# Low halves of the first three state-space input panels moved from GpSimd to VectorE

## The reference

```python
h = rmsnorm(x, norm_mix[l])
proj = h @ w_in[l]
(z, xbc, dt_raw, lru_y, lru_x, q, k, v, ret_g, gate_pre) = jnp.split(proj, offsets, axis=-1)
...
y_lru = rglru_mixer(lru_y, lru_x, ...)      # r, i = sigmoid(xb @ w_a), sigmoid(xb @ w_i); h = scan(a, u); h * gelu(y)
...
# ssd_mixer
xbc = jax.nn.silu(causal_dwconv(xbc, conv_w, conv_b))
```

## Time and profile before

| what | value |
| --- | --- |
| median of 3 runs | 2905.98 us (2905.45 to 2906.31) |
| the profiled execution | 2905.02 us, its span 2903.1 us |
| TensorE | 2878.9 us busy (99%), 17526 matmuls |
| VectorE | 2190.7 us busy (75%) |
| ScalarE | 1382.2 us busy (48%) |
| GpSimd | 396.9 us busy (14%) |

### The profile page before, as it was taken

How to read it: one execution, slowest core, us unless ns; L and a number is a source line. 1 busy time by engine, 2 the same in 40 slices (tenths; PEclk the granted TensorE clock), 3 DMA queues, 4 the chain that set the end, 5 groups by cost and what they waited for, 6 DMA issues and landing times.

```text
span 2903.1 us, 49040 instructions
## 1 busy us (share of the span) xinstructions
PE 2878.9 (99%) x17526; PEld 2533.8 (87%) x17526; DVE 2190.7 (75%) x3578; ACT 1382.2 (48%) x2252; POOL 396.9 (14%) x320
## 2 busy tenths in 40 slices
PE   9999999999999999999999999999999999999999
PEld 7888788778999888998887899988998887699987
DVE  8797574667999868887566888848889767688862
ACT  4653732344655525555233655525555236465541
POOL 0043240001111001110033011001110021011100
PEclk9999999999999999999999999999999999999999
DMA  3222123225677326773334477436773232257723
GB/s 139 100 92 91 66 94 116 73 80 181 156 184 180 89 94 181 181 180 100 109 109 131 128 180 181 113 116 178 185 182 106 103 115 74 81 157 183 183 78 109
DMA packets 143715, 375.93 MB, mean 129 GB/s; under 512 B 16144, under 2 KB 16400, under 8 KB 143184
## 3 DMA queue, kind: packets, MB, share of 16 engines
q1 hardware_dynamic: 110160, 309.44, 31.5%
q0 software_dynamic: 33408, 64.50, 13.1%
HBM read 371.78 MB, written 2.10 MB: 129 GB/s over the span
## 4 chain that ended last, share of the span: by engine, by line
PE 91%; DVE 6%; ACT 2%; issue 1%; DMA 1%; POOL 0%; SPq 0%; DVEq 0%; ACTq 0%; POOLq 0%
PE ps L1033 17%; PE ps L1035 17%; PE ps L1034 17%; PE ps L1487 12%; PE ps L1489 12%; PE ps L1488 12%; PE ps L1430 1%; DVE w_lo L2646 1%; DVE region_low L3216 0%; PE ps L1713 0%; PE ps L1750 0%; PE ps L1205 0%; DVE region_low L3589 0%; PE ps L1194 0%; PE ps L1419 0%
## 5 line engine op out<-in xcount | busy, mean ns | idle before, releaser
L1824 ACT ACTIVATE w_hi<-raw 128x1024 fp32r<-128x1024 f32 x300 | 315.8, 1055 | 284.3 <-DMA raw<-in_wstream 284.1
L1487 PE MATMUL ps<-h_hi,w_hi 128*128 128x256 f32 x1440 | 409.6, 284 | 1.1 <-DVE h_lo L3296 0.4
L1488 PE MATMUL ps<-h_lo,w_hi 128*128 128x256 f32 x1440 | 407.5, 283 | 0.0
L1033 PE MATMUL ps<-h_hi,w_hi 128*128 128x512 f32 (+1 forms) x883 | 347.4, 393 | 2.6 <-DVE w_lo L2646 1.8
L1035 PE MATMUL ps<-h_hi,w_lo 128*128 128x512 f32 (+1 forms) x883 | 340.7, 386 | 0.0
L1034 PE MATMUL ps<-h_lo,w_hi 128*128 128x512 f32 (+1 forms) x883 | 340.5, 386 | 0.0
L2646 DVE TENSOR_TENSOR w_lo<-raw,w_hi 128x1024 fp32r<-128x1024 f32 x220 | 265.7, 1220 | 84.7 <-ACT w_hi L1824 74.3
L1487 PEld LDWEIGHTS ps<-h_hi,w_hi 128*128 128x128 f32 x1440 | 276.1, 192 | 6.2 <-issue 1.6
L1488 PEld LDWEIGHTS ps<-h_lo,w_hi 128*128 128x128 f32 x1440 | 276.2, 192 | 0.5 <-issue 0.2
L937 POOL TENSOR_TENSOR w_lo<-raw,w_hi 128x1024 fp32r<-128x1024 f32 x78 | 195.2, 2508 | 496.6 <-ACT w_hi L1824 487.2
L1833 ACT ACTIVATE stage<-ps 128x512 f32<-128x512 f32 x107 | 63.4, 596 | 393.3 <-PE ps L1035 380.1
(11 more groups left out here) (694 smaller groups left out, 7635.7 us busy)
## 6 DMA issues: line engine op xcount, KB each, us to landing
raw<-in_wstream SPq DMA_DIRECT2D x301, 512.0 KB, 3.2
region<-in_pairs SPq DMA_DIRECT2D x193, 256.0 KB, 4.0
region<-in_pairs POOLq DMA_DIRECT2D x124, 256.0 KB, 5.5
region<-in_pairs SPq DMA_DIRECT2D x46, 512.0 KB, 5.8
last_pairs<-in_pairs SPq DMA_DIRECT2D x66, 256.0 KB, 4.0
raw<-in_pairs SPq DMA_DIRECT2D x22, 512.0 KB, 5.0
last_pairs<-in_pairs SPq DMA_DIRECT2D x22, 512.0 KB, 5.5
last_pairs<-in_pairs POOLq DMA_DIRECT2D x44, 256.0 KB, 5.5
```

The costliest lines, as they stand in the source:

```text
L1033: nc.tensor.matmul(dst, hi_w, hi_x, start=first, stop=False)
L1487: nc.tensor.matmul(dst, w1, x1, start=start, stop=False, skip_group_check=not first)
L1488: nc.tensor.matmul(dst, w1, x0, start=False, stop=False, skip_group_check=not first)
L1824: nc.scalar.activation(w_hi[:, n % HL], raw[:, r], ACT.Copy).then_inc(hi_ready, 1)
```

## The change

The first GpSimd run begins at panel 31 instead of 28. VectorE therefore makes the low halves of panels 28, 29 and 30. Because one pass of the `xbc` loop would then have panels of both makers, the three passes are written out on TensorE and on VectorE. ScalarE and SyncE have the same instructions as before.

```diff
-POOL_RUNS = {"first": (ST["xbc"].n, ST["br0"].n),
+POOL_RUNS = {"first": (ST["xbc"].n + 3, ST["br0"].n),
...
-            gemm("xbc", h_hi, h_lo)
+            gemm("xbc", h_hi, h_lo, groups=(0, 1, 2))
...
-            gemm("xbc", ssd_in, 3)
+            gemm("xbc", ssd_in, 3, groups=(0, 1, 2))
```

## The result

The changed kernel takes **2913.93 us** (median of 10 runs, 2911.49 to 2916.51), the kernel before 2906.31 us (10 runs beside them). The ratio is 1.0026, 95% interval 1.0018 to 1.0034: 7.6 us slower, just over the 0.2% that a measurement can tell. In a second series it took 2912.59 us (11 runs) against 2906.17, ratio 1.0023 (1.0014 to 1.0032). The forecast was 2914.0 us, in the range 2909.8 to 2916.0.

What follows compares the result with a forecast made beforehand. TensorE, busy 99% of the span, was taken as the bound. Panel 29's shift of +6.20, 0.17 for restarting and 1.7 for the clock sum to +8.07 on 2905.98: 2914.0 us, range 2909.8 to 2916.0.

Steps and rivals of the forecast that it cites:

- The old wait: TensorE's 1.77 us idle before panel 27, blamed on GpSimd's panel 28 lengthening VectorE's chain by 2.19 us; claimed to vanish.
- panel 28: Low half made by VectorE in the last block: ready at 163.70, wanted at 164.40, so hidden by 0.7 us.
- panel 29: Low half behind the recurrence's last result: VectorE's turn at 174.75, TensorE wants it at 169.84; the deciding term.
- The race: GpSimd's panel 32 asks at 174.62, VectorE's panel 29 at 174.75; GpSimd first by 0.13 us, a margin as large as the error.
- rival 1: VectorE's panel 29 goes ahead of GpSimd's panel 32: +4.25 + 1.7 = +5.95 us, 2911.9; chance 0.30.
- the forecast's case: GpSimd's panel 32 goes ahead of VectorE's panel 29: +6.37 + 1.7 = +8.07 us, 2914.0; chance 0.42.
- The clock term: TensorE's clock drops to the lower level after the new gap at panel 29: 1.7 us lost, ends 0 and 3.4.
- the restart: TensorE's slow restart after a wait, 0.17 us as seen at panel 27, added to panel 29's shift.
- The rival without a clock loss: TensorE's clock stays up after the gap at panel 29: +4.25 or +6.37 us, 2910.2 or 2912.3; chance 0.10.
- The prediction's row at 8.00: At 8.00 to 10.70 TensorE was busy 1.60 of 2.70 us, then granted clock 0.51 for 3.40 us: 1.7 us lost.
- Panel 30: Low half behind tile 0's convolution, 4.4 us after panel 29's, 6.5 with a lock; panel 29's 5.44 plus 1.7 hides it.
- Rival 3: Not slower: TensorE doesn't wait at panel 29 and the wait before panel 27 is gone: 2903.4 us; chance 0.06.

Runs made afterwards that it cites:

- The kernel with the loops alone: The kernel before with only the xbc loops written out on TensorE and VectorE, all low halves as before: 2906.78 us against 2906.25, ratio 1.0002.
- The forcing kernels: The changed kernel with panel 29's low half made to precede GpSimd's panel 32: 2912.19 us against 2906.30; with the order reversed: 2914.59 against 2906.17.
- the filled gap: The changed kernel with VectorE always first, plus 22 unused TensorE products ahead of its wait for panel 29: 2909.98 us against 2906.30, ratio 1.0015.

## Why the prediction came out as it did

**The mechanism was right.** The old wait went for the reason given (line 2976 at 0.69 us instead of 2.88), panel 28 was hidden (its low half began at 162.28, forecast 162.48), and panel 29 decided. VectorE's turn for it came at 174.45, forecast 174.75, or 174.56 with this execution's 0.19. The rest of the difference is mostly the one lock in this chain: priced at 2.13, it took 2.04 us (3.26 - 1.22). GpSimd asked at 168.96 and 174.45, forecast 169.1 and 174.62. Nothing later took the delay back. The kernel with the loops alone rules out the written-out code.

**The race was called the wrong way for the executions that the profiles show.** The forecast gave GpSimd the first place, by a margin of 0.13 us that it called as large as its error. All three profiles of the change have VectorE first, as in rival 1. In the first the margin was 0.00: the 0.09 us by which the lock was priced too high is most of the 0.13. The forcing kernels bracket it: +5.9 and +8.4 us against the +5.95 and +8.07 of the two cases. The median of the first series, +7.6, lies between them and nearer to the forecast's case, that of the second series, +6.4, nearer to rival 1. So that the first median came within 0.1 us of the forecast is partly luck: the case behind the number is not the one that the profiles show, and no profile shows what happened in the runs around that median.

**The clock term was right in kind and in range, on weak grounds.** It was set at 1.7 us, with ends at 0 and 3.4, plus 0.17 for the restart. From panel 29's start to the next wait it was 130.58 us before. The three profiles of the change have 133.18, 132.29 (174.41 to 306.70) and 132.22 (174.30 to 306.52), so they lose 2.60, 1.71 and 1.64 us. With VectorE forced first it is 132.83 (175.51 to 308.34), a loss of 2.25, and with GpSimd forced first 133.53 (178.12 to 311.65), a loss of 2.95. The low half of panel 29 moved early gives the smallest loss: from panel 30's start it was 125.14 us before (177.38 to 302.52) and is 126.64 (183.66 to 310.30), 1.50 more. The length of the gap doesn't order these losses: 2.95 stands behind 3.87 and 8.24 us, 1.50 behind 8.74, and 1.64 to 2.60 behind the same 5.91. What differs is how much of the time at 1.2 GHz falls on work. In the first profile the clock falls at about 174 and is back at 181.0, 5.3 us after panel 29's start, and half of that is 2.6. In the third it falls at about 171 and is back at 177.6, 3.3 us after the start, and half of that is 1.6. In the first profile 3.98 + 2.60 gives the whole 6.58. The rival without a clock loss is out: only the filled gap keeps its clock, and it is 2.2 us faster.

*TensorE: Matmul & The Clock Gate* of the Trainium skill ("Why this matters for your kernels") says that a long enough gap sends TensorE back to its throttled clock, and the traces agree (0.50 behind 3.87 us and more). The prediction's row at 8.00 was weaker evidence for it than I took it to be. These are TensorE's idle times in and just before that row, and at 985 to 989, in the kernel before:

```profile
8.87 0.47 PE L1033 MATMUL ps<-br_hi,w_hi 128*128 128x512 f32 x1 [1.36 <-DVE br_lo L2871]
...
10.04 0.50 PE L1033 MATMUL ps<-br_hi,w_hi 128*128 128x512 f32 x1 [0.24 <-DVE br_lo L2871]
...
988.66 0.50 PE L1033 MATMUL ps<-region_low,w_hi 128*128 128x512 f32 x1 [2.56 <-DVE region_low L3589]
```

The clock fell at 10.70 behind idle times of 1.36 and 0.24 us and stayed up behind 2.56. So the length of a gap alone doesn't tell the two rows apart, the row at 8.00 is no case of a long gap, and the 1.7 us taken from it were a guess at the price. That it came out inside 1.50 to 2.95 is in part luck.

**Panel 30** was hidden as forecast, but closely: the filled gap shows 0.24 us of wait once panel 29 runs at full clock.

**Rival 3** (not slower, since low halves are made faster on VectorE) fell. Each low half did take 1.22 instead of 2.4 us, and that was worth nothing against coming 5.9 us late. The *GPSIMD Engine Reference* of the Trainium skill ("Engine selection") advises giving two-input elementwise work to VectorE, since GpSimd is about twice as slow. The traces agree for the instruction (2.39 against 1.22 us), but here the order outweighed it.

## What to carry to other kernels

When work moves from a slow idle engine to a fast one, ask first where it will stand in that engine's order and when its result is wanted there; here 1.2 us saved per instruction cost 6 to 8 us of TensorE's time. A lock between two engines is felt at the place of the order where it falls, so removing one instruction moves the next one's lock onto other work: list what stands between each of them and the next result that somebody waits for. Add the clock to a new gap of TensorE as a term with its own spread: here the gaps of 3.87 us and more cost 1.5 to 3.0 us behind them.

## What the runs showed of the hardware

- The granted clock fell to 0.50 in gaps of 3.87, 5.91, 8.24 and 8.74 us of a TensorE that had been busy throughout; in the stretch of 985 to 989, with 2.56 us idle, it stayed at 1.00, and at 10.70 it fell behind idle times of 1.36 and 0.24 us. The work behind a gap lost 1.50 to 2.95 us, and the longer gap did not lose more.
- 22 products without a purpose in a gap of 5.91 us kept the clock at 1.00 and made the kernel with that gap 2.2 us faster.
- A GpSimd low half made the VectorE instruction that it met about 2.1 us longer, whatever that instruction was: 2.88 instead of 0.69 us for a root, 2.52 instead of 0.43 for a gate, 3.26 instead of 1.22 for a scan, 2.60 instead of 0.54 for a convolution's first instruction. GpSimd's own, behind VectorE's low half, took 3.46 instead of 2.39.
- Which row starts first doesn't tell who holds the lock. GpSimd's row at 152.86 is 0.06 us ahead of VectorE's at 152.92, and GpSimd was first; at 173.01 against 173.03 it is 0.02 ahead, and VectorE was first. The stretched duration tells it.
